# Activations with tokens in partitions: output stages that stream 512 weight columns, and norms per token tile

## The reference

```python
def rmsnorm(x, g):
    y = x32 * lax.rsqrt(jnp.mean(x32 * x32, axis=-1, keepdims=True) + EPS)
    return (y * g).astype(x.dtype)

def conv_ffn(h, w_in, w_conv, w_out):          # D_FF = 2816, conv of width 3 along the tokens
    u = h @ w_in
    ...
    gate, val = jnp.split(u, 2, axis=-1)
    return (jax.nn.silu(gate) * val) @ w_out

def trunk_layer(x, mod, g_mix_pre, g_mix_post, g_ffn_pre, g_ffn_post, w_ffn_in, w_ffn_conv, w_ffn_out, mixer):
    shift1, scale1, gate1, shift2, scale2, gate2 = mod
    h = rmsnorm(x, g_mix_pre) * (1 + scale1) + shift1
    y, ctx_state = mixer(h)
    x = x + gate1 * rmsnorm(y, g_mix_post)
    h = rmsnorm(x, g_ffn_pre) * (1 + scale2) + shift2
    x = x + gate2 * rmsnorm(conv_ffn(h, w_ffn_in, w_ffn_conv, w_ffn_out), g_ffn_post)
    return x, ctx_state
```

## Time and profile before

| | us |
|---|---|
| median of 3 runs | 1723.24 (1721.23 to 1725.34) |
| span of the profiled execution | 1720.7 |
| PE busy | 1601.5 (93%) |
| DVE busy | 1097.6 (64%) |
| ACT busy | 716.9 (42%) |
| output stages: mix of layer 0 and 1; each of the four of the feed-forward | 59.8 and 61.1; 77.6 |
| the three norms between stages | 51.3, 47.4, 46.2 |
| from the last matmul of the last output stage to the end | 20.4 |

### The profile page before, as it was taken

How to read it: one execution, slowest core, us unless ns; L and a number is a source line. 1 busy time by engine, 2 the same in 40 slices (tenths; PEclk the granted TensorE clock), 3 DMA queues, 4 the chain that set the end, 5 groups by cost and what they waited for, 6 DMA issues and landing times.

```text
span 1720.7 us, 31763 instructions
## 1 busy us (share of the span) xinstructions
PE 1601.5 (93%) x11837; PEld 1535.5 (89%) x11837; DVE 1097.6 (64%) x2060; ACT 716.9 (42%) x1189; POOL 132.3 (8%) x133
## 2 busy tenths in 40 slices
PE   7798998879999999999889979989799999999996
PEld 4797887869999999999879967779699999999996
DVE  5796766957777767778853248853666642466534
ACT  6532664264443134442251147652565531344410
POOL 1431110010000000000100032500100000000001
PEclk9898999999999999999999989999999999999998
DMA  9233002503334533345422120102022221222211
GB/s 362 83 127 106 2 2 92 193 10 117 115 112 165 177 120 110 110 144 188 147 80 73 62 65 2 45 7 80 13 75 81 79 85 61 71 73 74 91 67 61
DMA packets 43773, 160.33 MB, mean 93 GB/s; under 512 B 5184, under 2 KB 6208, under 8 KB 43440
## 3 DMA queue, kind: packets, MB, share of 16 engines
q1 hardware_dynamic: 40896, 152.00, 26.5%
q0 software_dynamic: 1584, 6.38, 1.1%
q10 hardware_dynamic: 1216, 0.92, 0.2%
HBM read 155.74 MB, written 3.54 MB: 93 GB/s over the span
## 4 chain that ended last, share of the span: by engine, by line
PE 76%; DVE 10%; issue 4%; ACT 2%; DMA 2%; POOL 0%; ACTq 0%; DVEq 0%; POOLq 0%; SPq 0%
PE ps L1498 28%; PE ps L1499 28%; PE ps L1676 4%; PE ps L1705 3%; PE ps L1533 3%; PE ps L1691 3%; DMA work<-in_wmodt 2%; DVE work L848 2%; PE ps L1625 1%; PE ps L1626 1%; DVE wlo L840 1%; DVE work L927 1%; DVE ring L848 1%; DVE x L961 1%; PE ps L1512 1%
## 5 line engine op out<-in xcount | busy, mean ns | idle before, releaser
L523 ACT ACTIVATE whi<-raw 128x1024 fp32r<-128x1024 f32 (+1 forms) x166 | 185.7, 1121 | 578.7 <-PE ps L1499 495.9
L1498 PE MATMUL ps<-hh,whi 128*128 128x320 f32 x928 | 288.7, 311 | 15.3 <-DVE wlo L840 15.3
L1499 PE MATMUL ps<-hh,whi 128*128 128x320 f32 x928 | 287.9, 310 | 0.0
L1498 PE MATMUL ps<-hl,whi 128*128 128x320 f32 x928 | 287.7, 310 | 0.0
L1499 PE MATMUL ps<-hl,whi 128*128 128x320 f32 x928 | 287.7, 310 | 0.0
L1499 PE MATMUL ps<-hh,wlo 128*128 128x320 f32 x928 | 287.7, 310 | 0.0
L1498 PE MATMUL ps<-hh,wlo 128*128 128x320 f32 x928 | 287.7, 310 | 0.0
L840 DVE TENSOR_TENSOR wlo<-raw,whi 128x1024 fp32r<-128x1024 f32 (+1 forms) x166 | 218.4, 1318 | 74.8 <-ACT whi L523 74.5
L1498 PEld LDWEIGHTS ps<-hh,whi 128*128 128x128 f32 x928 | 175.1, 189 | 17.1 <-DVE wlo L840 17.1
L1498 PEld LDWEIGHTS ps<-hl,whi 128*128 128x128 f32 x928 | 175.3, 189 | 0.0
L1499 PEld LDWEIGHTS ps<-hh,whi 128*128 128x128 f32 x928 | 175.2, 189 | 0.0
(11 more groups left out here) (219 smaller groups left out, 3169.6 us busy)
## 6 DMA issues: line engine op xcount, KB each, us to landing
raw<-in_w SPq DMA_DIRECT2D x134, 512.0 KB, 3.5
work<-in_wmodt SPq DMA_DIRECT2D x54, 512.0 KB, 3.6
raw<-in_w SPq DMA_DIRECT2D x32, 704.0 KB, 4.2
ring<-in_wmodt SPq DMA_DIRECT2D x26, 512.0 KB, 3.7
work<-in_wmod SPq DMA_DIRECT2D x16, 512.0 KB, 6.0
work<-in_rpb POOLq DMA_DIRECT2D x8, 448.0 KB, 4.2
x<-in_x SPq DMA_DIRECT2D x8, 320.0 KB, 6.6
out_x<-x SPq DMA_DIRECT2D x8, 320.0 KB, 2.2
```

The costliest lines, as they stand in the source:

```text
L523: nc.scalar.activation(whi[:, s, 0:kk * P], raw[:, s, 0:kk * P], ACT.Copy).then_inc(s_hi, 1)
L1498: T.matmul(bankA[s], slot(w, s, k), h[:, k, 0:HT], start=st, stop=sp_)
L1499: last = T.matmul(bankB[s], slot(w, s, k), h[:, k, HT:NT], start=st, stop=sp_)
```

## The change

`x` and `y` now have tokens in partitions: five tiles of 128 tokens (the fifth is the context), 1024 features wide. `h`, which the `in` and `fin` phases read, stays as it was.

- **Output stages.** The stationary operand is a chunk of activations, 128 features x 128 tokens; 512 columns of weights are streamed past it. A stage makes two halves of 512 output features; each half has five accumulators, one per token tile. The weights come in another order: a unit holds two chunks of 512 columns (one chunk in the first unit of each half in `fout`). `mix` has 8 units, `fout0` and `fout1` 12.
- **The last two units of the second half** are run tile by tile where a norm follows, so that tile 0 is complete first.
- **Norms.** ACT squares rows of a tile and sums them along the row in the same instruction; root and reciprocal are one value per token. DVE gates `y` with the gate as a row (`grow`, brought by two DMAs of POOL through DRAM), updates `x`, and scales `x` to the normed tile; PE transposes the tile in 8 blocks (`turn`); DVE (tiles 0, 3, 4) or ACT (tiles 1, 2) applies scale and shift; ACT makes the high part, DVE the remainder. Matrices of ones, spreads and POOL's additions go. At the entry of layer 1, `h` is written in another order of the tokens, in steps of 8 elements.
- **The first two units behind a norm** run in three pieces: tokens 0 to 255, 256 to 511, and 512 to 639.
- The start is done the same way (ACT squares and scales tiles, PE transposes them). `x` is stored as five tiles of 512 KB. The sums of the modulation's 80 blocks on DVE are dealt out anew over the units of layer 0, and SP's load loops are written out.

What PE does at the end of the mix of layer 0 and behind it, before: the last two matmuls of the stage, then sums of squares of `y`, the spread, sums of squares of `x`, the spread, and the first pair.

The core of the diff:

```diff
+CHUNKS_OF = {"mix": ((0, 1), (2, 3), (4, 5), (6, 7)),
+             "fout0": ((0,), (1, 2), (3, 4), (5, 6), (7, 8), (9, 10)),
+             "fout1": ((0,), (1, 2), (3, 4), (5, 6), (7, 8), (9, 10))}
...
-        x = sb("x", [P, KD, NT])
+        x = sb("x", [P, 5, D])
...
+            def square_x(b, t, out=None):
...
+                nc.scalar.activation(yt[:, t, :] if out is None else out, x[:, t, :], ACT.Square,
+                                     accum_out=acc_x[:, t:t + 1]).then_inc(s_sqx, 1)
...
+            def gate_mixed(b, half, t):
...
+                V.tensor_tensor(yt[:, t, 512 * half:512 * half + 512], y_bank(half, t),
+                                grow[:, stream(t), 512 * half:512 * half + 512], ALU.mult).then_inc(s_yf, 1)
...
+                V.scalar_tensor_tensor(out=x[:, t, :], in0=yt[:, t, :], scalar=inv_y[:, t:t + 1], in1=x[:, t, :],
+                                       op0=ALU.mult, op1=ALU.add).then_inc(s_xu, 1)
...
+                V.tensor_scalar(xn[t % 2], x[:, t, :], inv_x[:, t:t + 1], None, ALU.mult).then_inc(s_xn, 1)
...
+                for k in range(KD):
+                    last = V.tensor_scalar(hft[t % 2][:, k, :], turn_bank(t)[:, tile(k)],
+                                           coef[:, layer, which, st, k:k + 1],
+                                           mod_col(layer, 0 if which == 0 else 3, st)[:, k:k + 1], ALU.mult, ALU.add)
...
+                if b == 1 and t < 4:
+                    for r in range(2):
+                        last = V.tensor_tensor(columns_of(hl, 2 * t + r), hft[t % 2][:, :, 64 * r:64 * r + 64],
+                                               columns_of(hh, 2 * t + r).bitcast(F32), ALU.subtract)
...
-            def spread(n):
-
-                pe.wait_ge(s_rec, n + 1)
-                if n:
-                    pe.wait_ge(s_t, 8 * n)
-                for t in range(5):
-                    ins = T.matmul(inverse_rows[:, t * P:(t + 1) * P], std[:, t:t + 1].to_broadcast([P, P]), ident[:, :],
-                                   start=True, stop=True)
-                ins.then_inc(s_row, 1)
...
+            def tile_products(u, k, c, half, t, first, last):
+
+                s = u % 2
+                for n, (h, w) in enumerate(((hh, whi), (hh, wlo), (hl, whi))):
+                    ins = T.matmul(y_bank(half, t), h[:, k, tile(t)], w[:, s, c * 512:(c + 1) * 512],
+                                   start=first and n == 0, stop=last and n == 2)
...
+                        for t in range(2):
+                            for c, k in enumerate(before):
+                                products(u, k, c, half, t, False, False)
+                        pe.wait_ge(s_lo, u + 2)
+                        for t in range(5):
+                            if t >= 2:
+                                for c, k in enumerate(before):
+                                    products(u, k, c, half, t, False, False)
+                            for c, k in enumerate(final):
+                                ins = products(u + 1, k, c, half, t, False, k == last_k)
...
+            def boundary(b, u0):
+
+                yi = TOKEN_PHASES.index(NORMED[b])
+                for t in range(4):
+                    turn(b, t)
...
+                if b == 1:
+                    turn(b, 4)
+                    pe.wait_ge(s_tl, 5 * b + 4)
+                else:
+                    pe.wait_ge(s_afa, 2 * b + 1)
+                    pe.wait_ge(s_tl, 5 * b + 2)
+                piece(u0, 0, HF, 0, 0, True, True)
+                if b != 1:
+                    turn(b, 4)
+                pe.wait_ge(s_tl, 5 * b + 4)
+                pe.wait_ge(s_yf, 10 * yi + 10)
+                piece(u0, HF, NS, 1, 0, True, False)
+                pe.wait_ge(s_tl, 5 * b + 5)
+                piece(u0, NS, NT, 1, HF, False, True)
```

More of the change, by code:

```diff
@@ new lines, in piece @@
+            def piece(u0, c0, c1, bank, f, start, final):
+                for s in range(2):
+                    for k in range(KD):
+                        for n, (w, h) in enumerate(((whi, hh), (whi, hl), (wlo, hh))):
+                            last = T.matmul(ps[:, 2 * s + bank, f:f + c1 - c0], slot(w, s, k), h[:, k, c0:c1],
+                                            start=start and k == 0 and n == 0, stop=final and k == KD - 1 and n == 2)
+                    if c1 == NT:
+                        last.then_inc(s_unit, 1)
```

1428 lines of the change are left out of this document (835 added, 593 removed).

## The result

The kernel after takes 1665.81 us (median, 1663.96 to 1667.62), the kernel before 1722.30 us (1721.23 to 1725.34) in the same comparison: a ratio of 0.9664, with a 95% interval of 0.965 to 0.9678. The forecast was 1664, in a range of 1642 to 1688. The profiled execution has a span of 1662.2 us against 1720.7, so 58.5 us are to be placed; the forecast's sum was 59.3.

What follows compares the result with a forecast made beforehand. PE bounds the dense stages, engines waiting in series the norms; streaming -18.7, norms -35.1, end -11.3, start and modulation sums +5.8 give -59.3: 1720.7 becomes 1661.4, with 2.5 for the median 1664 us, range 1642 to 1688.

Steps and rivals of the forecast that it cites:

- Streaming, price: Output stages: 512 columns instead of 320 save each matmul's width-independent part, 0.2267 us per matmul, -18.7 us in all.
- rival (c): Output stages: a 512-wide matmul costs per column what a 320-wide does, so streaming gives nothing; 1678 us, chance 0.05.
- rival (d): Output stages: a matmul's fixed cost is the skill page's, about 2.5 ns; 1644 us, chance 0.03.
- Rival (e): Output stages: 512-wide matmuls with full stationary run as slowly as a plain fp32 row, 0.435 us each; 2036, chance 0.03.
- this sign of its being wrong: Stages: the prediction counts as wrong if PE waits in a stage for weights.
- Norms, size: Three norms between stages: tile-by-tile work shortens them by 14.6, 19.1 and 1.4 us, -35.1 in all.
- rival (a): Norms lighter: normalized tiles at half price, strided remainders at 1.2, less hand-over, no loss at the start; 1645, chance 0.18.
- the 1.3 us given to it: First piece behind a mix stage: 1.3 us lost on PE at a granted clock of 0.50.
- rival (b): Norms: ACT and DVE still take turns, each leaving an engine idle; norms 39, 39, 50 us; 1684, chance 0.14.
- Rival (f): Norms and end: no tile-wise overlap, tile 0's work starts only at the last matmul; 1698 us, chance 0.05.
- The end: Behind the last stage: only tile 4 is left at the last matmul, 9.1 us instead of 20.4, -11.3.
- The start: Before the first pair: ACT's added squares and scaled copies make its blocks 3.2 us, +5 us (0 to +7).

Runs made afterwards that it cites:

- light chunks: Kernel after, with the 20 modulation chunks summed during fout0 of layer 0 loaded for 64 of 1024 columns (sums then wrong): 1658.57 us.
- later write: Kernel after, with POOL writing the gate of layer 1's entry only from the sixth unit of layer 0's fin1 on: 1660.88 us.
- full price: Kernel after, with the normalized tile made by a two-tensor multiply (scalar broadcast along the row) instead of a per-partition scalar: 1673.31 us.

## Why the prediction was right, and where it was not

The time came within 2 us of the forecast. The mechanism was right for the price of streaming, for DVE's queue in the norms and for the end; it was wrong about the loads in layer 0, and at the start it is not shown. The sum is as close as it is by luck: two wrong terms cancel, 8.2 us lost in layer 0 against 8.9 gained in the norms.

- **Streaming, price.** Right to the digit: 0.227 apart, 74.83 us per stage where nothing disturbs. Splitting the columns measured the fixed cost at 13.5 ns, against rival (c), by which there is none. The 2.5 ns of the page of the Trainium skill that the prediction cites, rival (d), don't hold here. Rival (e), the slow 512-wide matmul, is refuted by the same starts.
- **Streaming, place.** The step that failed is the sentence "Loads, the unrolled queue of SP and the gates' way through DRAM cost nothing". It took 3.5 us per load as given and compared one load with one unit. In layer 0 a stage that should be 2.8 us shorter has the weights and the sums' chunks to bring beside it (DMA share 0.67 in fout0, 0.52 before), in fout0 even more chunks than before, and the gate's write stretches the loads next to it to 11 us. Neither the count of the chunks nor the write was priced. Layer 0's feed-forward stages gave +2.9 where -5.3 was forecast. Of these 8.2, the light chunks took back 2.4 inside fout0 and 2.1 of the gap of 3 behind it; the later write took back all of that gap (and 1.4 in fin1, whose start lay at the lower clock). The 2.3 in fout1, of which PE's waits show 1.1, have chunks beside them too, 14 where there were 16, but were not tried by themselves; their cause is not shown. The forecast named this sign of its being wrong, a wait in a stage for weights, and gave it no chance.
- **Norms, size.** -44.0 instead of -35.1. The largest part is the normalized tile, 0.69 from start to start instead of 1.15: the full price was measured at 6.5 us over the three norms. The forecast had this case as a part of its rival (a), and took the row of another form for its sum. The rule of the Trainium skill, by which the forecast had estimated 0.62, was the better guide. The strided remainder was 2.1 instead of 2.6 per tile, 2.0 in the norm into layer 1. Against these stand an affine of 2.64 instead of 2.1 per tile, and the third piece, 5.3 instead of 4.3.
- **Norms, clock.** Behind the mix stages the first piece ran at full clock (0.99), so the 1.3 us given to it were not spent there; the lower clock (0.50) fell on the transposes ahead of it, where the 16 from 350.27 take 3.3 us, 0.21 each, against 0.10 for the eight at 359.46. That this costs about as much, 1.7, is chance. A gain of 1.6 us in each of the fin0 phases was not forecast: before, the third unit began at the lower clock (0.63 over the first 4 us), now at 1.00.
- **Norms, mechanism.** DVE's queue was named as the bound. In the kernel after DVE works nearly without a gap from 332.7 to 352.6 in the first norm (19.5 of 19.9 us), and rival (b), turns between ACT and DVE with idle on both, did not come. But the queue is not the only bound: relieving it by 2.3 us gave nothing, since 1.1 to 1.2 of it became a wait for the high part of the same tile, and POOL's pass stretched what stood beside it.
- **Tile by tile.** Rival (f) priced the lack of it at 34 us (1698); the run without it took 26.4 more. The overlap was real. The price of (f) lies 1.6 to 1.9 above the run at each of the four places, since the run is not quite (f): there tile 0 is still complete ahead of the last matmul, and DVE's first gate stands 1.7 us ahead of it (340.48 to 342.21), against 8.3 in the kernel after (333.32 to 341.62).
- **The end.** 8.9 against 9.1: a store lands 2.7 us behind its issue, and each of the five hangs on one tile only.
- **The start.** +7.7 against +5, outside the bound of +7 in this execution. ACT's blocks do come 3.26 us apart (forecast 3.2), but ACT's work as the only reason did not hold; the rest stays open.
- **Slips in the sums.** Normalized tiles at 0.62 would have given 13 x 0.53 = 6.9 us, not 6.3; rival (c) comes out at 1679, not 1678; and the 2036 of rival (e) is a span, 2039 as a time. None changes the forecast.

## What to carry to other kernels

Streaming wider saves a fixed cost per matmul, so count matmuls, but look at once at what fed the stage beside it: a stage that becomes shorter keeps its bytes (fout0 of layer 0 was given more), and its loads can become the next thing that is late. A DMA that writes a few KB in 4-byte pieces belongs where nothing loaded beside it is due soon. For a norm in the open, the order in which the last tiles become complete ahead of it (26 of 56 us here) was worth as much as the rewrite of the norm itself.

## What the runs showed of the hardware

- Writing 8 KB to DRAM in 4-byte pieces took 9.1 to 12.8 us in the four places of the kernel after, and slowed 512 KB loads of another queue beside it from 3.6 to 11 us on average, up to 12.8. That the size of the pieces is the reason was not tried.
- A split-type matmul of 128 columns with its own stationary costs 0.111 us, one of 256 costs 0.120, one of 384 0.174, one of 512 0.227: between 128 and 256 columns the width hardly matters.
- A POOL pass over two SBUF tensors of 128 x 1024 takes 2.3 to 2.4 us and stretches the DVE instruction beside it from 0.765 to 2.17, or from 1.22 to 2.69; an affine of eight steps out of PSUM beside another pass kept its 2.64.
- A DVE multiplication of one fp32 SBUF tensor by a column of scalars takes 0.765 us for 1024 values, the same with the scalar as a broadcast tensor 1.22.
- Writing with a stride of 32 bytes costs DVE 1.09 per 512 elements instead of 0.69, and ACT 1.15 per 512 instead of some 0.6 (L698; the same ACT step takes 1.06 for 1024 in a row).
